# First block's local attention on TensorE: two heads of one key head per unit, or one head of each key head

## The reference, cut to what matters

```python
N_Q_HEADS, N_KV_HEADS, GQA_GROUP, WINDOW = 8, 2, 4, 128
qb = q.reshape(B, nb, C, N_KV_HEADS, GQA_GROUP, HEAD_DIM)      # nb = 4 blocks of C = 128 tokens
kk, vv = band(kb), band(vb)                                    # the block before, and this one
s = jnp.einsum('bnqhgd,bnkhd->bnhgqk', qb, kk) * HEAD_DIM ** -0.5
s = jnp.where(mask, s, -inf)
p = jax.nn.softmax(jnp.concatenate([s, sink], axis=-1), axis=-1)[..., :-1]
o = jnp.einsum('bnhgqk,bnkhd->bnqhgd', p, vv)
ya = o.reshape(B, S, ATT_Q) @ w_a
```

## Time and profile before

| | us |
|---|---|
| median of the runs shown (3) | 3352.75 (3350.56 to 3355.22) |
| the profiled execution's own time | 3352.07 |
| its span, from the first to the last instruction | 3350.3 |
| outside the span | 1.77 |
| mean granted TensorE clock | 0.992 |
| TensorE busy | 3298.9 (98%), 17250 instructions |
| VectorE / ScalarE / GpSimd busy | 1812.4 / 1283.0 / 1861.1 |

### The profile page before, as it was taken

One profiled execution on the slowest core, in us unless ns is written; L12 is line 12 of the kernel. 1 busy time (PEld: TensorE's weight loads), 2 busy tenths in 40 slices (PEclk: granted clock), 3 DMA queues, 4 the chain that ended last, 5 costly groups with the idle time before them and its releaser, 6 DMA issues.

```text
span 3350.3 us, 50242 instructions
## 1 busy us (share of the span) xinstructions
PE 3298.9 (98%) x17250; PEld 2751.5 (82%) x17250; DVE 1812.4 (54%) x2893; ACT 1283.0 (38%) x2071; POOL 1861.1 (56%) x2076
## 2 busy tenths in 40 slices
PE   8999999999999999999999999899999999999999
PEld 6778888888777888888888878899998888788887
DVE  4543258778544237778856445566652664442113
ACT  4433342224344233323444553343343445543223
POOL 5325568887434557888565223456554463246555
PEclk9999999999999999999999999999999999999999
DMA  4213345554322335555353113112222442233333
GB/s 173 82 51 95 100 134 182 174 170 143 112 70 62 96 96 179 172 176 188 109 138 96 45 51 101 57 57 69 75 63 64 130 118 75 64 107 107 98 96 107
DMA packets 106428, 358.54 MB, mean 107 GB/s; under 512 B 12000, under 2 KB 22496, under 8 KB 104352
## 3 DMA queue, kind: packets, MB, share of 16 engines
q1 hardware_dynamic: 71712, 257.13, 24.1%
q10 hardware_dynamic: 34560, 99.30, 9.2%
HBM read 336.79 MB, written 8.59 MB: 103 GB/s over the span
## 4 chain that ended last, share of the span: by engine, by line
PE 63%; POOL 16%; issue 16%; DVE 3%; ACT 1%; DMA 1%; POOLq 0%; ACTq 0%; DVEq 0%; SPq 0%
POOL w_lo L652 16%; PE ps L1121 6%; PE ps L1120 6%; PE ps L1122 6%; PE ps L775 4%; PE ps L776 4%; PE ps L777 4%; PE ps L1338 3%; PE ps L1339 3%; PE ps L1340 3%; PE ps L1029 2%; PE ps L1030 2%; PE ps L1031 2%; PE ps L1176 2%; PE ps L1178 2%
## 5 line engine op out<-in xcount | busy, mean ns | idle before, releaser
L652 POOL TENSOR_TENSOR w_lo<-w_raw,w_hi 128x256 fp32r<-128x256 f32 x1904 | 1700.2, 925 | 1348.2 <-ACT w_hi L1711 1334.3
L1711 ACT ACTIVATE w_hi<-w_raw 128x1024 fp32r<-128x1024 f32 x448 | 473.1, 1056 | 661.7 <-DMA w_raw<-in_w 190.6
L775 PE MATMUL ps<-h_hi,w_hi 128*128 128x512 f32 x944 | 373.5, 396 | 0.0
L776 PE MATMUL ps<-h_lo,w_hi 128*128 128x512 f32 x944 | 368.8, 391 | 0.0
L777 PE MATMUL ps<-h_hi,w_lo 128*128 128x512 f32 x944 | 368.8, 391 | 0.0
L2654 DVE SCALAR_TENSOR_TENSOR ada_junk<-ada_w,c_silu 128x1024 f32<-128x1024 f32 x192 | 320.5, 1669 | 3.3
L1338 PE MATMUL ps<-c_hi,w_hi 128*128 128x512 f32 (+1 forms) x832 | 299.1, 359 | 4.8 <-DVE vm L2913 3.2
L1339 PE MATMUL ps<-c_lo,w_hi 128*128 128x512 f32 (+1 forms) x832 | 286.8, 345 | 0.0
L1340 PE MATMUL ps<-c_hi,w_lo 128*128 128x512 f32 (+1 forms) x832 | 286.7, 345 | 0.0
L1120 PE MATMUL ps<-c_hi,w_hi 128*128 128x512 f32 (+1 forms) x792 | 279.5, 353 | 2.5 <-DVE c_lo L2825 2.5
L1121 PE MATMUL ps<-c_lo,w_hi 128*128 128x512 f32 (+1 forms) x792 | 278.6, 352 | 0.0
(11 more groups left out here) (421 smaller groups left out, 6650.5 us busy)
## 6 DMA issues: line engine op xcount, KB each, us to landing
w_raw<-in_w SPq DMA_DIRECT2D x476, 512.0 KB, 3.5
ada_w<-in_ada ACTq DMA_DIRECT2D x96, 512.0 KB, 3.6
zs<-stage ACTq DMA_DIRECT2D x52, 128.0 KB, 2.1
m_row<-m_spill ACTq DMA_DIRECT2D x16, 384.0 KB, 5.5
wq_row<-wq_spill ACTq DMA_DIRECT2D x16, 384.0 KB, 5.4
x_spill<-x ACTq DMA_DIRECT2D x2, 2048.0 KB, 8.1
zs_m<-zm ACTq DMA_DIRECT2D x32, 128.0 KB, 2.1
bias<-in_rpb ACTq DMA_DIRECT2D x8, 512.0 KB, 3.7
```

Source lines behind the costliest of these rows:

```text
L652: last = nc.gpsimd.tensor_tensor(w_lo[:, j, c], w_raw[:, j % RAW, c], w_hi[:, j, c].bitcast(F), ALU.subtract)
L775: nc.tensor.matmul(bank, w_hi[:, j, w], rhs_hi[:, k, :], start=(k == 0), stop=False)
L776: nc.tensor.matmul(bank, w_hi[:, j, w], rhs_lo[:, k, :], start=False, stop=False)
L1711: nc.scalar.activation(w_hi[:, j, :], w_raw[:, j % RAW, :], ACT.Copy).then_inc(hi_ready, 1)
```

## The change

A unit becomes a query block n and an index i from 0 to 3: it takes head i (key head 0) and head i + 4 (key head 1), which lie in one tile of `aq`, in its two halves of partitions. There are 16 units still. The two score matmuls lie in different halves of the array's rows and write banks 4 and 5; both banks belong to every unit, so `scores(u)` now waits for `s_done` of the unit before. The weighted sum becomes, per block of keys, two matmuls of 128 columns, for the two halves of bank 7's partitions. `scores(1)` moves behind `half(0, 1)`. The output copies take 128 partitions of 128 columns in place of 64 of 256.

```diff
-        units = [(n, g, i) for n in range(TT) for g in range(ATT_GROUPS) for i in range(2)]
+        units = [(n, i) for n in range(TT) for i in range(ATT_HEADS // ATT_GROUPS)]
...
                 def scores(u):
-                    n, g, i = units[u]
-                    rows = slice(g * HEAD, (g + 1) * HEAD)
+                    n, i = units[u]
                     keys = slice(max(n - 1, 0) * P, (n + 1) * P)
                     wide = keys.stop - keys.start
-                    for e in range(2):
-                        last = nc.tensor.matmul(ps[:, 4 + u % 2, e * 2 * P:e * 2 * P + wide], aq[rows, 2 * i + e, n * P:(n + 1) * P],
-                                                ak[rows, keys], start=True, stop=True)
+                    if u:
+                        pe.wait_ge(s_done, l * N_ATT + u)
+                    for g in range(ATT_GROUPS):
+                        rows = slice(g * HEAD, (g + 1) * HEAD)
+                        last = nc.tensor.matmul(ps[:, 4 + g, 0:wide], aq[rows, i, n * P:(n + 1) * P], ak[rows, keys], start=True, stop=True)
                     last.then_inc(sc_ready, 1)
...
                     first = 0 if n else 1
                     for b in range(first, 2):
-                        last = nc.tensor.matmul(ps[g * HEAD:(g + 1) * HEAD, 7, 0:2 * P],
-                                                av[:, n - 1 + b, g * HEAD:(g + 1) * HEAD], pt_sb[:, u % 2, b, :, :],
-                                                start=(b == first), stop=(b == 1))
+                        for g in range(ATT_GROUPS):
+                            rows = slice(g * HEAD, (g + 1) * HEAD)
+                            last = nc.tensor.matmul(ps[rows, 7, 0:P], av[:, n - 1 + b, rows], pt_sb[:, u % 2, b, g, :],
+                                                    start=(b == first), stop=(b == 1))
                     last.then_inc(pv_ready, 1)
...
                 scores(0)
+                half(0, 1).then_inc(chunk_used, 1)
                 scores(1)
-                half(0, 1).then_inc(chunk_used, 1)
                 pe.wait_ge(v_done, l + 1)
...
-                    nc.scalar.activation(o_hi[rows, 2 * i:2 * i + 2, n * P:(n + 1) * P],
-                                         ps[rows, 7, 0:2 * P].rearrange("p (e q) -> p e q", e=2), ACT.Copy).then_inc(ohi_ready, 1)
+                    nc.scalar.activation(o_hi[:, i, n * P:(n + 1) * P], ps[:, 7, 0:P], ACT.Copy).then_inc(ohi_ready, 1)
...
-                    nc.vector.tensor_tensor(o_lo[at], ps[rows, 7, 0:2 * P].rearrange("p (e q) -> p e q", e=2),
-                                            o_hi[at].bitcast(F), ALU.subtract).then_inc(olo_ready, 1)
+                    nc.vector.tensor_tensor(o_lo[at], ps[:, 7, 0:P], o_hi[at].bitcast(F), ALU.subtract).then_inc(olo_ready, 1)
...
-                    nc.vector.scalar_tensor_tensor(s_sb[:, u % 2, :, 0:wide], ps[:, 4 + u % 2, :].rearrange("p (e k) -> p e k", e=2)[:, :, 0:wide],
+                    nc.vector.scalar_tensor_tensor(s_sb[:, u % 2, :, 0:wide], ps[:, 4:6, 0:wide],
                                                    inv_now[:, 1, n:n + 1], att_mask[:, :, 2 * P - wide:2 * P], ALU.mult, ALU.add).then_inc(s_done, 1)
```

More of the change, by code:

```diff
@@ L862, in scores @@
                 def scores(u):
-                    n, g, i = units[u]
-                    rows = slice(g * HEAD, (g + 1) * HEAD)
+                    n, i = units[u]
                     keys = slice(max(n - 1, 0) * P, (n + 1) * P)
                     wide = keys.stop - keys.start
-                    for e in range(2):
-                        last = nc.tensor.matmul(ps[:, 4 + u % 2, e * 2 * P:e * 2 * P + wide], aq[rows, 2 * i + e, n * P:(n + 1) * P],
-                                                ak[rows, keys], start=True, stop=True)
+                    if u:
[3 more added lines that the diff above has]
+                        last = nc.tensor.matmul(ps[:, 4 + g, 0:wide], aq[rows, i, n * P:(n + 1) * P], ak[rows, keys], start=True, stop=True)
                     last.then_inc(sc_ready, 1)
                 def weighted(u):
-                    n, g, i = units[u]
+                    n = units[u][0]
                     pe.wait_ge(pt_copied, l * N_ATT + (u + 1))
@@ L2482, in output_lower @@
                 def output_lower(u):
-                    n, g, i = units[u]
-                    rows = slice(g * HEAD, (g + 1) * HEAD)
-                    at = (rows, slice(2 * i, 2 * i + 2), slice(n * P, (n + 1) * P))
+                    n, i = units[u]
+                    at = (slice(0, P), i, slice(n * P, (n + 1) * P))
                     dve.wait_ge(ohi_ready, l * N_ATT + (u + 1))
-                    nc.vector.tensor_tensor(o_lo[at], ps[rows, 7, 0:2 * P].rearrange("p (e q) -> p e q", e=2),
-                                            o_hi[at].bitcast(F), ALU.subtract).then_inc(olo_ready, 1)
+                    nc.vector.tensor_tensor(o_lo[at], ps[:, 7, 0:P], o_hi[at].bitcast(F), ALU.subtract).then_inc(olo_ready, 1)
                 def take(i):
@@ L2508, in _ @@
                 for u in range(N_ATT):
-                    n, g, i = units[u]
+                    n, i = units[u]
                     wide = 2 * P if n else P
-                    c, h = tiny[:, u % 2, :], 4 * g + 2 * i
+                    c, heads = tiny[:, u % 2, :], slice(i, i + 5, 4)
                     dve.wait_ge(sc_ready, l * N_ATT + (u + 1))
@@ L2519, in _ @@
                     dve.wait_ge(mx_done, l * (2 * N_ATT) + (2 * u + 1))
-                    nc.vector.scalar_tensor_tensor(c[:, 0:2], c[:, 12:14], -1.0, sink_now[:, 1, h:h + 2], ALU.mult, ALU.min).then_inc(mx_done, 1)
+                    nc.vector.scalar_tensor_tensor(c[:, 0:2], c[:, 12:14], -1.0, sink_now[:, 1, heads], ALU.mult, ALU.min).then_inc(mx_done, 1)
                     dve.wait_ge(mx_done, l * (2 * N_ATT) + (2 * u + 2))
-                    nc.vector.tensor_tensor(c[:, 2:4], c[:, 0:2], sink_now[:, 0, h:h + 2], ALU.add).then_inc(nm_ready, 1)
+                    nc.vector.tensor_tensor(c[:, 2:4], c[:, 0:2], sink_now[:, 0, heads], ALU.add).then_inc(nm_ready, 1)
                     if u == 1:
```

## The result

| | before | after |
|---|---|---|
| median of the runs | 3353.15 (3350.56 to 3355.22, 4 runs) | 3335.32 (3333.19 to 3335.65, 4 runs) |
| the profiled execution's own time | 3352.07 | 3333.19 |
| its span | 3350.3 | 3331.4 |
| stretch of layer 1, layer 2 (first score to first retention matmul) | 135.87, 135.89 | 125.95, 125.94 |
| first score to first transpose, layer 1, layer 2 | 7.48, 7.50 | 8.96, 8.96 |

The ratio is 0.9945 (95% interval 0.9931 to 0.996): faster by 0.55%. Predicted were 3333.2, 3329 to 3342. The experiments are held against the 3333.20. They ran in three sets; the kernel before, run beside each, had medians of 3352.97, 3352.64 and 3353.61, so a difference of 1 us between two sets means nothing.

A forecast was written before the change was run, and what follows sets the result against it. TensorE was taken to bound both attention stretches; per layer 4.9 + 0.4 (scores) + 5.0 + 0.8 (weighted sums) - 1.5 (start), taken as 9.8, 19.6 in two layers, gave 3352.75 - 19.6 = 3333.2 us, range 3329 to 3342.

The forecast's parts named there:

- Scores: Score matmuls: two heads overlap fully, 0.64 us instead of 1.05, and 0.42 instead of 0.63 for n = 0.
- Weighted sums: Weighted-sum matmuls: two heads overlap fully, 0.58 us instead of 1.00, and 0.36 instead of 0.57 for n = 0.
- The new wait for `s_done`: Wait ahead of scores(u): costs nothing; for u = 1 a half of 2.95 us covers DVE's instruction of 0.48.
- `scores(1)` behind the half: Start of each layer's units: TensorE goes on 1.5 us later and then waits about 2.2 us; 3.0 in the kernel.
- The 2.19: Time in us from DVE's start on unit 1 until TensorE goes on, assumed unchanged at the start of the units.
- DVE, ACT and what is late next: Output copies sit beside TensorE's work; slack before the tightest step's transposes falls from 1.8 to about 0.9 us, staying positive.
- Rival 2: DVE's chain sets the pace in steps with turns, so transposes wait: at most 3346, likelier 3340; chance 0.07.
- rivals 3 and 4: No overlap, only the start's cost, 3356.6, chance 0.03; doubled weight loads slow the weighted sums, 3376, chance 0.02.
- The sum: All terms together: 9.6 to 10.0 us saved per layer, taken as 9.8, 19.6 in two layers, giving 3333.2.
- there is no reason in the rows for another clock level: TensorE's wait of about 2.2 us at the start of the units was expected to leave the clock unchanged.

The follow-up runs named there:

- e2_order_back: Changed kernel with the old order put back, scores(1) ahead of half(0, 1): 3328.39 us, ratio 0.9926.
- e5_scores_twice: Changed kernel with every score matmul issued twice, same operands and result: 3350.33 us, ratio 0.9991.
- e8_after_again: Changed kernel run once more, unchanged: 3333.20 us, ratio 0.994.
- e4_heads_in_turn: Changed kernel with the weighted sum's two loops exchanged, one head's passes after the other's: 3334.15 us, ratio 0.9939.
- e10_order_split_late: e1_before_order with ACT's split of the last key and value chunk moved from its step 0 to step 1: 3360.12 us, ratio 1.0019.
- e7_values_and_first: e3_values_early with DVE also scaling unit 0's probabilities before it takes unit 1's scores: 3326.29 us, ratio 0.9919.
- e3_values_early: Changed kernel with DVE's values by token moved to its step 0, ahead of unit 1's scores: 3328.58 us, ratio 0.9925.
- e1_before_order: Kernel before the change with only scores(1) moved behind half(0, 1): 3363.08 us, ratio 1.0027.
- e9_order_busy: e1_before_order with twelve unread matmuls of 512 columns placed in TensorE's wait for av: 3356.63 us, ratio 1.0008.

## Why the prediction was right, point by point

- *Scores*: 0.63 and 0.42 to 0.43, predicted 0.64 and 0.42. *Weighted sums*: 0.59 and 0.37, predicted 0.58 and 0.36. Taking the second block's groups of the same form rather than a bound from the block itself was what made each of these terms right to about a hundredth.
- *The new wait for `s_done`*: no such wait in the profile, as predicted, and `e2_order_back` shows 0.59 where the cover is taken away. The half that covers it, put at 2.95 though the two times given beside it are 3.0 apart, took 2.94 (62.19 to 65.13).
- *`scores(1)` behind the half*: TensorE restarts 6.11 us after the first score (61.76 to 67.87), before 4.65; the 1.46 answer to the 1.5 predicted, the wait of 2.25 to "about 2.2". `e2_order_back` gives 1.50 a layer. Part of this is luck. The 2.19 stood because GpSimd's subtractions began at 67.03, when DVE's second tiny instruction (66.84, 0.16 long) had just ended; in `e5_scores_twice`, with DVE's scores 0.44 later, they met, and the wait grew to 3.32. The prediction didn't look at GpSimd there.
- *DVE, ACT and what is late next*: nothing waits for the copies or for `p_sb`; `e5_scores_twice` shows TensorE's time passed on in full. The smallest slack is 1.48, where the prediction had about 0.9: it was right in sign and too small. Rival 2 falls, and with the weighted sums at 0.59 so do rivals 3 and 4.
- *The sum*: 9.92 and 9.95 in the two layers against 9.8. The median predicted, 3333.2, is 2.1 below that of the four runs and 0.6 below that of all nine; it agrees with the five of `e8_after_again`. Since code that the change doesn't touch varies by more than this from one execution to the next, agreement to a tenth is luck. The stretches are what confirms the mechanism.

One sentence of it was wrong: "there is no reason in the rows for another clock level". In both profiled executions of the changed kernel it held, but in `e4_heads_in_turn` and `e10_order_split_late` a wait of the same length brought the clock down in both layers, for about 1.5 us each. How often that happens in timed runs of the changed kernel is open; its nine times spread over 4.2 us, those of `e7_values_and_first`, which has no such wait, over 1.3, but those of `e3_values_early`, which has none either, over 5.4, so the spread doesn't tell. And the same term, taken for the kernel before in `e1_before_order`, was short by 2.5 a layer: I had carried 2.19 us of DVE's and TensorE's work from the earlier trace rows to another moment without asking what GpSimd does at that moment.

## What to carry to other kernels

When two small matmuls are to share the array, the price is best read from a group of the same form that already alternates between halves elsewhere in the kernel, from its start to its follower's. Where a step is moved to hide a new wait, price the move against the wait: here the moved order was 1.5 us a layer slower than the one that pays a wait of 0.59, and with another place for DVE's `values_by_token` the moved order costs nothing. A duration carried to another moment holds only if the engines that slowed it, or didn't, do the same there: read all engines' rows at the new moment.

## What the runs showed of the hardware that I had not expected

- **DVE's instructions with two SBUF operands stand behind GpSimd's.** 0.16 us alone, 0.58 to 0.74 in most cases beside GpSimd's subtractions of 0.69 (2.77 for four), 0.15 to 0.35 in a few; DVE's scores and `av`, which read PSUM, keep 0.48 and 0.69 at either time. The Trainium skill, page "SBUF — State Buffer", section "Who interferes with whom", has a DVE instruction with two SBUF inputs contend with a GpSimd instruction that reads SBUF: the trace agrees. DVE's scaling of the probabilities (L2479), whose one wide operand is `p_sb`, is slowed too: two instructions take 0.48 alone and 1.22 beside the subtractions in the changed kernel, 1.29 in `e3_values_early`. The reciprocal (0.17) is not.
- **The clock can fall behind a wait of 2.24 us.** Profiled, two layers each: behind 2.24 to 2.25 us it fell in `e4_heads_in_turn` and `e10_order_split_late` and not in the changed kernel and `e8_after_again`; behind 2.66 to 3.32 us it fell in `e1_before_order` and in `e5_scores_twice`; where the wait at the start of the units was under 0.6 it never fell there. What decides at 2.24 is open. A fall costs 1.3 to 1.6 us ahead of the first transposes, and in `e9_order_busy` unread matmuls in the wait prevented it.
- **The order of the passes in the program makes no difference to the overlap of the two halves**: eight take 0.59 us alternating and 0.60 with one head behind the other. This was tried for the weighted sums only.
